# Three of the twelve modulation steps in the first layer's attention computed on VectorE, inside the loop over the heads

## The reference

```python
cond_lat = jax.nn.silu(c)
for i in range(DEPTH):
    mod_l = (cond_lat @ w_mod[i] + b_mod[i])[:, None, :]
    sh1, sc1, g1, sh2, sc2, g2 = jnp.split(mod_l, N_MOD, axis=-1)
    a_lat = _modulate(x, norm_mix_g[i], sh1, sc1)      # _rmsnorm(x, g) * (1 + scale) + shift
    ...
        y_lat, y_ctx = _mla(a_lat, a_ctx, pos, ctx_out, ...)    # first layer: 8 heads
    ...
    x = x + g1 * y_lat
    f_lat = _modulate(x, norm_ffn_g[i], sh2, sc2)
    ...
        y = _hier_moe(tokens, *moe_args)               # 32 experts, 6 MB of weights each
        x = x + g2 * y[:B * S].reshape(B, S, D)
```

## Time and profile before

| | |
|---|---|
| median of 3 runs | 2130.47 us (2122.25 to 2131.82) |
| the profiled execution, its time | 2123.99 us |
| its span in the trace | 2122.2 us |
| TensorE busy | 2025.2 us, 95% of the span |
| VectorE busy | 1147.2 us, 54% |
| moved by DMA | 621.07 MB, mean 293 GB/s |

### The profile page before, as it was taken

How to read it: one execution, slowest core, us unless ns; L and a number is a source line. 1 busy time by engine, 2 the same in 40 slices (tenths; PEclk the granted TensorE clock), 3 DMA queues, 4 the chain that set the end, 5 groups by cost and what they waited for, 6 DMA issues and landing times.

```text
span 2122.2 us, 30652 instructions
## 1 busy us (share of the span) xinstructions
PE 2025.2 (95%) x13002; PEld 1440.6 (68%) x13002; DVE 1147.2 (54%) x1872; ACT 760.0 (36%) x1129; POOL 215.9 (10%) x187
## 2 busy tenths in 40 slices
PE   5999999999998999999999999898999999999998
PEld 3856644444443896444444339886999999999998
DVE  3844533332321755333332228887599766778983
ACT  4333211111111542111111118767455454445452
POOL 0000000000000000000000000024146200003640
PEclk9999999999999999999999999999999999999999
DMA  9789899999999868999999995454455555335552
GB/s 349 281 295 360 323 419 423 424 422 422 424 422 417 309 226 341 423 423 423 422 423 423 422 384 191 160 166 153 145 173 174 185 175 136 105 117 174 172 182 95
DMA packets 211372, 621.07 MB, mean 293 GB/s; under 512 B 16224, under 2 KB 99488, under 8 KB 161824
## 3 DMA queue, kind: packets, MB, share of 16 engines
q1 hardware_dynamic: 206528, 613.09, 74.8%
q10 hardware_dynamic: 4704, 5.98, 1.0%
HBM read 617.95 MB, written 1.08 MB: 292 GB/s over the span
## 4 chain that ended last, share of the span: by engine, by line
PE 68%; DMA 16%; DVE 9%; ACT 4%; SPq 2%; issue 1%; POOL 0%; DVEq 0%; ACTq 0%
PE bank L797 28%; PE bank L1623 15%; DMA ring<-in_moe_w_up 11%; PE bank L1632 7%; PE bank L785 3%; DMA normed<-in_moe_w_up 3%; DVE ring_rounded L333 2%; PE bank L1602 2%; PE bank L1639 2%; ACT ring_rounded L327 2%; PE bank L569 1%; DMA ring<-in_mla_w_dq 1%; DVE arena L2910 1%; SPq L304 1%; PE bank L1139 1%
## 5 line engine op out<-in xcount | busy, mean ns | idle before, releaser
L797 PE MATMUL bank<-normed_rounded,ring_rounded 128*128 128x256 f32 x3424 | 418.4, 284 | 3.6 <-DVE arena L2864 2.9
L797 PEld LDWEIGHTS bank<-normed_rounded,ring_rounded 128*128 128x128 f32 x3424 | 412.7, 190 | 6.9 <-DVE arena L2864 3.1
L1623 PE MATMUL bank<-ring,arena 128*64 128x512 f32 x1536 | 349.9, 593 | 18.6 <-DMA ring<-in_moe_w_up 18.5
L333 DVE TENSOR_TENSOR ring_rounded<-ring,ring_rounded 128x4096 fp32r<-128x4096 f32 (+2 forms) x64 | 277.9, 4343 | 100.8 <-ACT ring_rounded L327 100.8
L797 PE MATMUL bank<-arena_rounded,ring_rounded 128*128 128x256 f32 (+1 forms) x2288 | 291.8, 286 | 5.4 <-DVE arena_rounded L1436 3.2
L797 PEld LDWEIGHTS bank<-arena_rounded,ring_rounded 128*128 128x128 f32 x2288 | 280.1, 189 | 9.7 <-DVE arena_rounded L1436 3.9
L1623 PEld LDWEIGHTS bank<-ring,arena 128*64 128x64 f32 x1536 | 114.8, 137 | 238.8 <-issue 236.8
L2044 DVE TENSOR_TENSOR arena<-arena,bank 64x512 f32<-64x512 f32 x64 | 43.5, 680 | 364.8 <-ACT arena L1841 364.8
L327 ACT ACTIVATE ring_rounded<-ring 128x4096 fp32r<-128x4096 f32 (+2 forms) x64 | 220.5, 3446 | 36.0 <-DMA ring<-in_ffn_w_down 32.5
L2037 DVE SCALAR_TENSOR_TENSOR arena_rounded<-bank,arena,arena_rounded 64x512 fp32r<-64x512 f32 x128 | 96.0, 750 | 225.6 <-ACT arena_rounded L1857 223.5
L1632 PE MATMUL bank<-ring,arena 128*64 128x512 f32 x768 | 175.5, 598 | 1.9 <-ACT arena L1848 1.9
(11 more groups left out here) (318 smaller groups left out, 2443.8 us busy)
## 6 DMA issues: line engine op xcount, KB each, us to landing
ring<-in_moe_w_up SPq DMA_DIRECT2D x96, 1024.0 KB, 25.1
ring<-in_moe_w_gate SPq DMA_DIRECT2D x96, 1024.0 KB, 23.6
ring<-in_moe_w_down SPq DMA_DIRECT2D x96, 1024.0 KB, 23.8
ring<-in_ffn_w_up SPq DMA_DIRECT2D x44, 1024.0 KB, 6.9
ring<-in_w_mod SPq DMA_DIRECT2D x20, 2048.0 KB, 13.0
ring<-in_ssm_w_in SPq DMA_DIRECT2D x12, 2048.0 KB, 8.0
ring<-in_ffn_w_down SPq DMA_DIRECT2D x10, 2048.0 KB, 7.9
arena<-in_moe_w_gate SPq DMA_DIRECT2D x16, 1024.0 KB, 23.9
```

Source lines behind the costliest of these rows:

```text
L333: e.tensor_tensor(ring.rounded[slot][:, 0:n].bitcast(F32R), ring.slots[slot][:, 0:n], ring.rounded[(self.number + 1) % RING][:, 0:n], ALU. ...
L797: end = e.matmul(out, lhs.bitcast(F32R), rhs.bitcast(F32R), start=start and n == 0 and k == 0, stop=stop and n == 2 and k == n_k - 1)
L1623: ends[i] = e.matmul(bank[rows, :], xt[:, n * KD // 2 + j, :], weights[:, j, :], start=n == 0 and j == 0, stop=n == 1 and j == KD // 2 - 1)
```

## The change

Steps 7, 8 and 9 of layer 1 leave the packed steps, which are nine now, and form a second `SummedSteps`, `self.summed_late`. Its three sums lie in the second half of the columns of the normed buffer `k.A`, which nothing uses at that time. VectorE adds the first of them up after the softmax in head 1, the second in two halves in heads 3 and 4, the third in two halves in heads 5 and 6 (`self.sums_at`). The table `at_head` spreads the nine packed steps as 1, 1, 1, 2, 1, 2, 1, 0 over the heads, where it was 2, 2, 1, 2, 2, 1, 2, 0. SyncE fetches the chunks in another order. In head 7 TensorE makes the product with ones and the transposes for the three sums, and the gain of layer 1 is finished in `close_vector`.

```diff
@@ -476,10 +476,11 @@
 
 class SummedSteps:
 
-    def __init__(self, k, layer, first, sums, rows):
-        self.k, self.layer, self.first, self.sums, self.rows = k, layer, first, sums, rows
-        assert len(sums) == 4
-        self.chunks = [modulation_chunk(k, layer, first + n, k.dve) for n in range(4)]
+    def __init__(self, k, layer, first, sums, rows, before=None):
+        self.k, self.layer, self.first, self.sums, self.rows, self.before = k, layer, first, sums, rows, before
+        self.steps = len(sums)
+        assert self.steps <= 4
+        self.chunks = [modulation_chunk(k, layer, first + n, k.dve) for n in range(self.steps)]
 
     def fetch(self, e, w, n):
         self.chunks[n].fetch(e, w)
@@ -490,12 +491,14 @@
         w.wait_ge(*chunk.landed())
         w.wait_ge(*k.act.at("silu cond"))
         (weights,) = chunk.raw()
+        if len(total.shape) == 3:
+            weights = weights.rearrange("p k (a b) -> p k a b", a=total.shape[1])
         for i in tiles:
             if i == 0:
-                e.tensor_scalar(total, weights[:, i, :], k.silu_cond[:, i, 0:1], None, ALU.mult).then_inc(*dve.up())
+                e.tensor_scalar(total, weights[:, i], k.silu_cond[:, i, 0:1], None, ALU.mult).then_inc(*dve.up())
             else:
                 w.wait_ge(*dve.now())
-                e.scalar_tensor_tensor(total, weights[:, i, :], k.silu_cond[:, i, 0:1], total, ALU.mult, ALU.add
+                e.scalar_tensor_tensor(total, weights[:, i], k.silu_cond[:, i, 0:1], total, ALU.mult, ALU.add
                                        ).then_inc(*dve.up())
         if tiles[-1] == KD - 1:
             dve.mark("free", chunk.number)
@@ -505,7 +508,7 @@
         k = self.k
         bank, emptied = k.banks.next(k.act, "step sums", self.layer)
         w.wait_ge(*emptied)
-        w.wait_ge(*k.dve.at("step sum", self.layer, 3))
+        w.wait_ge(*k.dve.at("step sum", self.layer, self.steps - 1))
         for n, total in enumerate(self.sums):
             end = e.matmul(bank[32 * n:32 * n + 32, :], k.mat("ones")[:, 0:32], total, start=True, stop=True)
         end.then_inc(*k.pe.up("step sums", self.layer))
@@ -513,23 +516,29 @@
     def rows_scalar(self, e, w):
         k = self.k
         w.wait_ge(*k.pe.at("step sums", self.layer))
-        e.activation(self.rows, k.banks.of("step sums", self.layer)[:, :], ACT.Copy).then_inc(*k.act.up("step sums", self.layer))
+        if self.before:
+            w.wait_ge(*k.pe.at("turned sums", self.before.layer))
+        e.activation(self.rows[0:32 * self.steps, :], k.banks.of("step sums", self.layer)[0:32 * self.steps, :], ACT.Copy).then_inc(*k.act.up("step sums", self.layer))
 
     def turn_tensor(self, e, w):
-        k = self.k
+        k, rows = self.k, 32 * self.steps
         bank, emptied = k.banks.next(k.dve, "turned sums", self.layer)
         w.wait_ge(*emptied)
         w.wait_ge(*k.act.at("step sums", self.layer))
         for t in range(4):
-            end = k.turn(e, bank[:, t * P:(t + 1) * P], self.rows[:, t * P:(t + 1) * P])
+            end = k.turn(e, bank[:, t * P:t * P + rows], self.rows[0:rows, t * P:(t + 1) * P], rows)
         end.then_inc(*k.pe.up("turned sums", self.layer))
 
     def close_vector(self, e, w):
-        k, tiles = self.k, slice(4 * self.first, 4 * self.first + 16)
+        k, dve, tiles = self.k, self.k.dve, slice(4 * self.first, 4 * (self.first + self.steps))
         w.wait_ge(*k.pe.at("turned sums", self.layer))
-        by_step = k.banks.of("turned sums", self.layer)[:, :].rearrange("p (t n c) -> p n t c", t=4, c=32)[:, :, :, 0]
+        by_step = k.banks.of("turned sums", self.layer)[:, :].rearrange("p (t n c) -> p n t c", t=4, c=32)[:, 0:self.steps, :, 0]
         out, bias = (x.rearrange("p (n t) -> p n t", t=4) for x in (k.mod[:, self.layer, tiles, 0], k.col("b_mod")[:, self.layer, tiles]))
         e.tensor_tensor(out, by_step, bias, ALU.add).then_inc(*k.dve.up("turned sums", self.layer))
+        if tiles.start <= 4 * KD and 5 * KD <= tiles.stop:
+            w.wait_ge(*dve.now())
+            e.scalar_tensor_tensor(k.gain[:, self.layer, 1, :, 0], k.mod[:, self.layer, 4 * KD:5 * KD, 0], 1.0,
+                                   k.col("norm_ffn")[:, self.layer, :], ALU.add, ALU.mult).then_inc(*dve.up("gain", self.layer, 1))
 
 
 class PackedSteps:
@@ -1030,9 +1039,13 @@
         late = k_flat(self.PT[1])
         self.first = Modulation(k, 0, 0, 4, lambda at: early[at % 2])
         self.summed = SummedSteps(k, 0, 4, [*early, late[:, 0:512], late[:, 512:1024]], tables_both)
-        steps = [(0, 8), (0, 9), *((1, at) for at in range(10))]
+        behind = [k.A[:, 2 * n:2 * n + 2, SEQ:2 * SEQ] for n in range(3)]
+        self.summed_late = SummedSteps(k, 1, 7, behind, tables_both, self.summed)
+        steps = [(0, 8), (0, 9), *((1, at) for at in range(7))]
         self.packed = PackedSteps(k, steps, ar.take(KD, 2 * len(steps) + 30), k.rstd[:, :])
-        self.at_head = {0: (0, 1), 1: (2, 3), 2: (4,), 3: (5, 6), 4: (7, 8), 5: (9,), 6: (10, 11), 7: ()}
+        self.at_head = {0: (0,), 1: (1,), 2: (2,), 3: (3, 4), 4: (5,), 5: (6, 7), 6: (8,), 7: ()}
+        self.sums_at = {1: (0, range(0, KD)), 3: (1, range(0, 4)), 4: (1, range(4, KD)),
+                        5: (2, range(0, 4)), 6: (2, range(4, KD))}
 
         self.w_dq = k.weights("w_dq", a["mla_w_dq"][0], KD, 0, MLA_Q_LORA)
         wd = a["mla_w_dkv"][0].rearrange("(k p) n -> p k n", p=P)
@@ -1069,10 +1082,12 @@
         moe = self.later[0]
         moe.open_areas()
         moe.fetch_halves(e, w, 0, 1)
-        for first in range(0, 12, 4):
+        late, packed = self.summed_late, self.packed
+        for four in (((late, 0), (packed, 0), (packed, 1), (packed, 2)), ((late, 1), (packed, 3), (packed, 4), (packed, 5)),
+                     ((packed, 6), (packed, 7), (late, 2), (packed, 8))):
             pass_slots(2)
-            for n in range(first, first + 4):
-                self.packed.fetch(e, w, n)
+            for steps, n in four:
+                steps.fetch(e, w, n)
         self.w_o[0].fetch(e, w)
         moe.fetch_halves(e, w, 1, 5)
         pass_slots(2)
@@ -1214,10 +1229,13 @@
                 self.packed.step_tensor(e, w, n)
             if h == 0:
                 self.summed.sums_tensor(e, w)
+            if h == MLA_HEADS - 1:
+                self.summed_late.sums_tensor(e, w)
             turns(h)
             if h == 1:
                 self.summed.turn_tensor(e, w)
             if h == MLA_HEADS - 1:
+                self.summed_late.turn_tensor(e, w)
                 self.packed.turn_tensor(e, w)
             if h:
                 values(h - 1)
@@ -1320,6 +1338,8 @@
                 exps(h + 1)
             if h == 0:
                 self.summed.rows_scalar(e, w)
+            if h == MLA_HEADS - 1:
+                self.summed_late.rows_scalar(e, w)
             turned(h)
             if h == MLA_HEADS - 2:
                 self.packed.rows_scalar(e, w)
@@ -1456,6 +1476,9 @@
                 key_part(h + 2)
             if h + 1 < MLA_HEADS:
                 softmax(h + 1)
+            if h in self.sums_at:
+                self.summed_late.step_vector(e, w, *self.sums_at[h])
+        self.summed_late.close_vector(e, w)
         self.packed.close_vector(e, w)
         values(last - 1)
         values(last)
```

## The result

The changed kernel took 2139.94 us (median of 5 runs, 2137.24 to 2141.47) against 2129.11 us before (5 runs, 2122.25 to 2131.82). The ratio is 1.0057, with a 95% interval of 1.0038 to 1.0075: 12 us slower, between 8 and 16 (the two medians lie 10.8 us apart). The profiled execution took 2137.24 us, with a span of 2135.4 us, 13.2 us more than the span of before.

A forecast was written before the change was run, and what follows sets the result against it. TensorE and the DMA stream, both running without a gap, were taken to bound the heads. 4.2 us saved on TensorE, all spent in waits, and +13 us from two holes, from a mean of 2127.1, gave 2140 us; range 2127 to 2151.

The forecast's parts named there:

- TensorE's queue gets shorter, and the saving is spent in waits for chunks: Attention heads: 4.2 us less work on TensorE, all of it spent waiting for packed chunks.
- VectorE has the room: Attention heads: three summed steps, 17.9 us of added work, cost nothing because VectorE is busy 28.23 of 70 us.
- The first hole, 10.4 us: Stream of the heads: a fetch waits until the first late sum ends at 140.9 us, leaving a 10.4 us hole.
- The second hole, 12.0 us: Stream of the heads: a fetch waits for the second late sum, ending at 174.5 us, leaving a 12.0 us hole.
- the term that I had put between 0 and 2 and taken as 0: TensorE in the heads: a lower granted clock after its waits for chunks, 0 to 2 us, taken as 0.
- `w_o[0]` lands at 204.1 us: End of the heads: the projection's first weight chunk lands at 204.1 us, where by count it landed at about 181.7.
- The slack of 9.8 us: Between landing and rounding of `w_o[0]`: 9.8 us of slack covers that much of the 22.4 us of holes.
- The projection ends 13 us later: Output projection after the heads: one run of matmuls, 22.9 us, ending 12.9, say 13 us later.
- The signs: Profile after: two stretches without traffic, two SyncE waits of 10 us or so, TensorE waits, VectorE waiting some 12 us.
- B: Rival for the whole kernel: not slower, TensorE's gain stays and fetches find slots in time, 2123 us; chance 0.12.
- C: Rival in the stream of the heads: only one hole, costing 1 to 3 us, 2129 us; chance 0.14.
- D: Rival in the heads: two holes plus slower engines (clock or strided sums), 18 to 24 us, 2148 us; chance 0.10.

The follow-up runs named there:

- e1: The changed kernel with the first late chunk (summed on VectorE) fetched last in its round instead of first; 2131.26 us, ratio 1.0020 to the kernel before.
- e2: The changed kernel with all three late chunks (summed on VectorE) fetched last in their rounds; 2120.39 us, ratio 0.9970 to the kernel before.
- e6: The changed kernel with the three late sums taking only two of their eight tiles, fetches unchanged; 2133.61 us, ratio 1.0029 to the kernel before.
- e7: The changed kernel with the first late sum one head later, behind the softmax of head 3; 2150.64 us, ratio 1.0114 to the kernel before.
- e3: The kernel before, with three of twelve packed steps multiplying only one of their eight tiles on TensorE; 2121.89 us, ratio 0.9976.
- e4: The kernel before, with the 24 instructions of the three late sums added on VectorE, on a constant, result unread; 2128.82 us, ratio 1.0012.
- e8: The changed kernel with the late chunk first in the first fetch round, last in the other two; 2127.22 us, ratio 1.0000 to the kernel before.

## Why the prediction was right

The mechanism was right: e1, e2, e6 and e7 show it from several sides. That 2140 us was met to the tenth, at 2139.94, is luck. The forecast was 13 us on top of 2127.1; measured were 10.8 us between the medians, 12 by the ratio, on top of 2129.11. Point by point:

*TensorE's queue gets shorter, and the saving is spent in waits for chunks.* Right. The waits for p3 and p4 were forecast at 2.5 and 3.6 us, and measured 2.13 and 3.89; behind the second hole came three more, of 3.98, 1.95 and 2.13 us. That TensorE's work was worth something at all, e3 shows.

*VectorE has the room.* Right (e4: the rounding of `w_o[0]` did not come later, and all of the added work cost 0.2 to 4.7 us). The sum in two pieces of 256 costs nothing extra: seven multiply-adds took 5.47 us, against 5.48 in the earlier trace rows.

*The first hole, 10.4 us.* The forecast counted a hole as what lies between two landings beyond the 5.4 us of a chunk; the lost traffic above is about 1 us more. By the forecast's count the first hole was 9.4 us: the fetch ahead of it landed at 132.8 us (8.8 us from its issue) and S2 at 147.6 (7.8 from its issue). S2's fetch left at 139.84 instead of 140.9 us, because everything was 1.1 us early in this execution already, as the fetch of p2 shows (123.99 against 125.05 us in the earlier trace rows).

*The second hole, 12.0 us.* By the same count 14.2: p5 landed at 165.2 us and p6 at 184.8. The sum ended at 176.8 instead of 174.5 us. Most of the difference is the term that I had put between 0 and 2 and taken as 0: after its waits TensorE ran the step p4 in 3.64 us instead of 1.8, at 1.2 GHz. The window around it has a granted clock of 0.50:

```profile
155.00:160.00 5.00, 1.11 (x12) 0.09 (x8) 0.93 (x2) 0.00 (x0) 0.00 (x0) 0.50 1.05 387
```

Of this term I had taken the wrong end.

*`w_o[0]` lands at 204.1 us.* It landed at 207.5 (21.0 us from its issue at 186.51), and ScalarE took it at 207.49: 2.3 us from p6, which landed that much later than forecast, and 1.1 by which the count of chunks at 5.4 us is short over such a distance, as it was for `w_o[1]` in the kernel before.

*The slack of 9.8 us covers part of it.* Right, but it was 8.6: before, `w_o[0]` landed at 182.9 us (8.5 from its issue at 174.33), not at the 181.7 of the count, and was taken at 191.48. The landing moved by 24.6 us and the rounding by 16.0, the difference being this slack. In e1 the two are 17.2 and 8.6 us. e8 does not bear on it, since its chain went another way.

*The projection ends 13 us later.* It ended 14.85 us later, in an execution that was 1.1 us early ahead of the first hole, and though the rounding was 16.0 late: its run of 185 matmuls took 22.17 us instead of 23.32, at a granted clock of 1.00 instead of 0.94 (before, the clock was low at its beginning, 0.71 in 200 to 205 us). *The experts carry this to the end.* Right, and shown by the issues at 251.96 and 268.31 us; the details are in the last section. The 13.2 us by which the spans differ are made up of parts that the sum did not have: 14.85 us at the projection, 1.5 us more up to the first expert, and 3.2 us given back behind it.

*The signs.* The stretches without traffic, TensorE's waits and VectorE's 12.5 us ahead of the softmax of head 7 came where they were forecast. SyncE's two waits for VectorE in the heads were 15.6 and 27.5 us instead of 10 or so.

*The rivals.* B, not slower, is what happens when the fetches find their slots (e2, e3). C, one hole at 1 to 3 us, was measured at 0 (e8) and 4.3 (e1). D's slower clock was real and cost some 2 us on the way to p6; D had put the total at 18 to 24 us.

*The rule on the most contended engine.* The Trainium skill's page "Perfetto Trace Analysis" (Identifying the Most-Contended Engine) judged the DMA to be the more contended in the heads, by its measure correctly: 389 GB/s. By that rule the saving on TensorE would be worth nothing even without the holes. e3 contradicts that reading, with 3.0 to 7.4 us gained by work taken off TensorE alone. A stream that runs at its full rate, but ahead of its use, does not set the end.

## What to carry to other kernels

When an operation moves to another engine, ask what it frees as well as what it costs. Where fetches are issued in order into slots, the last reader of a slot decides when all later fetches leave, so a chunk with a late reader belongs last in its round: this order alone was worth some 19 us here, with the same work on every engine. The late chunk itself then comes last, and what needs its result can become the chain that ends last, as in `e2_late_last`. And a hole in a saturated stream must be counted against the slack of what stands behind it, the time between landing and use, and not against the engine's waits near it.

## What the runs showed of the hardware that I had not expected

TensorE's clock falls at places that differ between executions of almost the same work. The 32 small matmuls of the experts' routing (128x36) are the clearest place. In the kernel before they took 4.84 us in the first layer and 6.69 in the second, in the kernel after 6.35 and 4.84. The chain of waits of the kernel before has:

```profile
231.53 4.84 PE bank L1664 x32
```

```profile
807.25 6.69 PE bank L1664 x32
```

and that of the kernel after:

```profile
246.38 6.35 PE bank L1687 x32
```

```profile
821.47 4.84 PE bank L1687 x32
```

Single matmuls of this group take 279 ns or 408 ns, and the granted clock of the 5 us around is near 1.00 or 0.50 (2.4 or 1.2 GHz). TensorE did not stand still when it fell: in 810 to 815 us of the kernel before it was busy for all 5 us, at 0.50. In the first layer this makes 1.5 of the 16.35 us by which the first expert is late. In the second layer it turns round and gives 1.9 us back, part of the 2.3 us by which the shift falls from the end of the first expert stage to the end of the second (15.73 us at the fetch of `conv_w_out`, 752.81 against 768.54, and 13.47 at the first of `ssm_w_in`, 1269.96 against 1283.43). A difference of some 2 us between two single executions of this kernel should not be explained by the change.
